# Two token streams across the passages between the big products, squares summed on GpSimd, norm roots taken on columns

## What is computed

```python
# two layers i; the context stream xc does the same in layer 0
hl = modulate(rmsnorm(xl, g_pre_mix[i]), ml[0], ml[1])       # before w_in
xl_new = xl + ml[2] * rmsnorm(y_l, g_post_mix[i])             # y_l = merged @ w_o
h2 = modulate(rmsnorm(xl_new, g_pre_mlp[i]), ml[3], ml[4])    # before w_mlp_in ("up")
xl_new = xl_new + ml[5] * rmsnorm(sqrelu_mlp(h2, ...), g_post_mlp[i])
# third block
h = rms_norm(x, norm1_g); z = h @ w_in                        # "win2"
x = x + merged @ w_o                                          # "w_o2"
x = x + peer(rms_norm(x, norm2_g), peer_wq, ...)              # "wq2"
```

## Time and profile before

| | us |
|---|---|
| median of 3 runs | 4296.63 (4293.73 to 4300.03) |
| profiled execution | 4287.48 |
| its span | 4286.2 |
| PE busy | 3978.9 |
| DVE busy | 2143.3 |
| ACT busy | 1532.8 |
| POOL busy | 494.4 |

### The profile page before, as it was taken

How to read it: one execution, slowest core, us unless ns; L and a number is a source line. 1 busy time by engine, 2 the same in 40 slices (tenths; PEclk the granted TensorE clock), 3 DMA queues, 4 the chain that set the end, 5 groups by cost and what they waited for, 6 DMA issues and landing times.

```text
span 4286.2 us, 47339 instructions
## 1 busy us (share of the span) xinstructions
PE 3978.9 (93%) x19554; PEld 3173.2 (74%) x19554; DVE 2143.3 (50%) x3759; ACT 1532.8 (36%) x1878; POOL 494.4 (12%) x748
## 2 busy tenths in 40 slices
PE   6988989999889889998798999999998999999999
PEld 4755768888766668875676877878877788888887
DVE  2165343333447344453353343788883566654444
ACT  3245442212234542234455333344444322222222
POOL 0000000000000000000000100176566111100000
PEclk8999999999999899998899999999999999999999
DMA  5400113332120022222111432344555656643332
GB/s 192 165 8 1 52 70 115 118 109 98 50 81 1 16 74 89 99 79 93 53 47 61 134 109 87 139 155 142 176 167 163 200 182 193 189 143 127 109 117 89
DMA packets 109831, 459.73 MB, mean 107 GB/s; under 512 B 9216, under 2 KB 43120, under 8 KB 68912
## 3 DMA queue, kind: packets, MB, share of 16 engines
q1 hardware_dynamic: 82048, 354.96, 23.8%
q0 software_dynamic: 27568, 101.74, 8.1%
HBM read 389.04 MB, written 67.63 MB: 107 GB/s over the span
## 4 chain that ended last, share of the span: by engine, by line
PE 81%; DVE 7%; ACT 6%; DMA 3%; POOL 2%; issue 2%; SPq 0%; DVEq 0%; ACTq 0%; POOLq 0%
PE ps L538 21%; PE ps L540 21%; PE ps L539 21%; PE ps L951 2%; PE ps L2257 2%; PE ps L618 2%; PE ps L968 1%; POOL Y L2393 1%; PE ps L471 1%; DMA gdram<-GST 1%; DVE MX L1111 1%; PE ps L957 1%; PE ps L1014 1%; DMA stage<-in_w_mod 1%; PE ps L1805 1%
## 5 line engine op out<-in xcount | busy, mean ns | idle before, releaser
L538 PE MATMUL ps<-HH,WH 128*128 128x512 f32 x2760 | 1062.1, 385 | 56.4 <-DVE HL L659 38.0
L539 PE MATMUL ps<-HL,WH 128*128 128x512 f32 x2760 | 1051.9, 381 | 0.0
L540 PE MATMUL ps<-HH,WL 128*128 128x512 f32 x2760 | 1051.6, 381 | 0.0
L445 DVE TENSOR_TENSOR WL<-stage,WH 128x2048 fp32r<-128x2048 f32 x248 | 567.7, 2289 | 488.1 <-ACT WH L434 488.1
L434 ACT ACTIVATE WH<-stage 128x2048 fp32r<-128x2048 f32 x248 | 472.8, 1906 | 589.6 <-PE ps L540 533.3
L538 PEld LDWEIGHTS ps<-HH,WH 128*128 128x128 f32 x2760 | 526.5, 191 | 169.5 <-issue 53.0
L540 PEld LDWEIGHTS ps<-HH,WL 128*128 128x128 f32 x2760 | 526.5, 191 | 106.5
L539 PEld LDWEIGHTS ps<-HL,WH 128*128 128x128 f32 x2760 | 525.8, 191 | 103.6 <-issue 0.7
L538 PE MATMUL ps<-AHp,WH 128*128 128x512 f32 x1024 | 406.8, 397 | 7.3 <-ACT Y L2575 7.3
L539 PE MATMUL ps<-ALp,WH 128*128 128x512 f32 x1024 | 406.6, 397 | 0.0
L540 PE MATMUL ps<-AHp,WL 128*128 128x512 f32 x1024 | 406.5, 397 | 0.0
(11 more groups left out here) (360 smaller groups left out, 5072.2 us busy)
## 6 DMA issues: line engine op xcount, KB each, us to landing
stage<-in_w SPq DMA_DIRECT2D x64, 1024.0 KB, 4.9
stage<-in_u SPq DMA_DIRECT2D x64, 1024.0 KB, 4.9
stage<-in_v SPq DMA_DIRECT2D x64, 1024.0 KB, 4.9
stage<-in_w_mod SPq DMA_DIRECT2D x48, 1024.0 KB, 4.9
GR<-gdram POOLq DMA_DIRECT2D x32, 1024.0 KB, 8.4
adram<-GR SPq DMA_DIRECT2D x22, 1024.0 KB, 4.2
AR<-adram POOLq DMA_DIRECT2D x88, 256.0 KB, 3.5
gdram<-GST SPq DMA_DIRECT2D x16, 1024.0 KB, 5.7
```

Source lines behind the costliest of these rows:

```text
L445: dve.e.tensor_tensor(k.WL[o % 2][:, 0:w], k.stage[n % 2][:, 0:w], k.WH[o % 2][:, 0:w].bitcast(F32), ALU.subtract).then_inc(*dve.done("sla ...
L538: pe.e.matmul(o, wh[:, kk, cs], L.hh[:, kk, z], start=first, stop=False)
L539: pe.e.matmul(o, wh[:, kk, cs], L.hl[:, kk, z], start=False, stop=False)
L540: mm = pe.e.matmul(o, wl[:, kk, cs], L.hh[:, kk, z], start=False, stop=last)
```

## The change

A class `Bridge` describes a passage, and a list of steps (`mlp_steps`, `x_steps`, `p_steps`) gives its order; every engine walks through the same list and does its own part of each step. The tokens go in two streams: latents and context in layer 0, two halves of 256 in layer 1 and later. The last two slabs of the product before (`last=2`) and the first two of the one after (`first=2`) are computed chunk by chunk for one stream, then for the other; `out (c, s)` and `in (c, s)` are such chunks. ScalarE squares as before, but sums of squares go to GpSimd for every norm of the passages (`pool_square_sum`, line 968 of the changed kernel). The statistics are products of the sum with one column of ones, giving a column per 128 tokens (step `stat`, line 869); ScalarE takes one Sqrt over these 2 or 4 columns (`root`, line 898), VectorE the reciprocal, and puts it on a diagonal (`diag`); a product of ones with the diagonal (`rows`, line 874) brings the factors to all partitions in PSUM, where the add and split steps read them. `hi` and `lo` are the splits of the next matrix's slabs. `add (s, c)` multiplies chunk c and adds chunk c - 1; `split` likewise. GpSimd's loads in `pool_heads` wait for the last norm before `win2`. Modulation slabs are not woven into `up`'s group 0, layer 1's scales are computed before the passage into its `w_in`, `HH2` and `HL2` lie elsewhere in SBUF, and the PSUM banks are handed between rings of four double banks and of eight single ones. The core of the diff:

```diff
+STREAMS = [[LAT, CTX], [(0, 256), (256, 256)]]
...
+        def streamed(chunks):
+            for s, z in enumerate(self.streams):
+                for c in chunks:
+                    if any(s0 <= z[0] < s0 + sn for s0, sn in self.segs(c)):
+                        yield (c, s), c, s
+
+        yield from streamed(range(self.first))
+        for c in range(self.first, self.last):
+            yield c, c, None
+        yield from streamed(range(self.last, self.n))
...
-            woven(("up", l, g), 2, lambda s: io["w1"][l, 2 * g + s], rest, lambda s: 1)
+            woven(("up", l, g), 2, lambda s: io["w1"][l, 2 * g + s], rest, lambda s: 1 if g > 0 else 0)
...
+            for i in L.used_after(key):
+                scalar_split(k, act, k.slab_of[L.name, i] + 2)
...
-def vector_square_sum(k, dve, name, c, a, b):
-    t, before = k.TA.of((name, c)), k.TA.of((name, c - 1))
-    dve.wait_ge("square", (name, c))
-    if c > 1:
-        dve.wait_ge("sq_sum", (name, c - 1))
-    dve.e.tensor_tensor(t[:, a:b], t[:, a:b], before[:, a:b], ALU.add).then_inc(*dve.done("sq_sum", (name, c)))
...
+def steps(name, *xs):
+    return [(name, x) for x in xs]
+def add_steps(s, lo=0, hi=9):
+    return steps("add", *[(s, c) for c in range(lo, hi)])
+def split_steps(s, lo=0, hi=9):
+    return steps("split", *[(s, c) for c in range(lo, hi)])
+def second_half(l, adds):
+    y1, n0, n1 = ("y", 1), ("n", 0), ("n", 1)
+    use = lambda *cs: steps("use", *[(c, 0) for c in cs]) if l == 0 else []
+    if l == 0:
+        out = adds[:-2] + steps("stat", y1) + steps("root", y1) + adds[-2:] + steps("hi", 1) + steps("lo", 0)
+        out += steps("diag", y1) + steps("rows", y1) + steps("lo", 1)
+        out += steps("stat", n0) + steps("root", n0) + steps("diag", n0) + steps("rows", n0)
+    else:
+        out = adds + steps("hi", 1) + steps("lo", 0) + steps("stat", n0) + steps("root", n0) + steps("diag", n0)
+        out += steps("stat", y1) + steps("root", y1) + steps("diag", y1) + steps("rows", n0, y1)
+    out += split_steps(0) + steps("in", (0, 0), (1, 0)) + (steps("lo", 1) if l == 1 else []) + add_steps(1)
+    out += use(0, 1) + steps("in", (2, 0)) + steps("stat", n1) + steps("root", n1) + steps("diag", n1) + use(2)
+    return out + steps("in", (3, 0)) + steps("rows", n1) + split_steps(1) + use(3)
+def mlp_steps(l):
+    y0 = ("y", 0)
+    out = steps("out", (4, 0), (5, 0), (6, 0), (7, 0), (4, 1)) + steps("stat", y0) + steps("root", y0) + steps("diag", y0)
+    out += steps("out", (5, 1)) + steps("rows", y0) + steps("out", (6, 1)) + add_steps(0, 0, 3) + steps("hi", 0)
+    return out + steps("out", (7, 1)) + steps("made", 0) + second_half(l, add_steps(0, 3))
+def x_steps(l):
+    y0 = ("y", 0)
+    out = steps("out", *[(c, 0) for c in range(8)], (0, 1), (1, 1)) + steps("stat", y0) + steps("root", y0)
+    out += steps("diag", y0) + steps("out", (2, 1), (3, 1)) + steps("rows", y0)
+    for c in range(4):
+        out += steps("out", (4 + c, 1)) + add_steps(0, c, c + 1) + (steps("hi", 0) if c == 1 else [])
+    return out + steps("made", 0) + second_half(l, add_steps(0, 4))
+def p_steps():
+    n0, n1 = ("n", 0), ("n", 1)
+    out = steps("out", (4, 0), (5, 0), (6, 0), (7, 0), (4, 1)) + steps("stat", n0) + steps("root", n0) + steps("diag", n0)
+    out += steps("out", (5, 1)) + steps("rows", n0) + steps("out", (6, 1)) + steps("hi", 0) + split_steps(0, 0, 2)
+    out += steps("lo", 0) + steps("out", (7, 1)) + steps("made", 0) + steps("hi", 1) + split_steps(0, 2)
+    out += steps("stat", n1) + steps("root", n1) + steps("diag", n1) + steps("lo", 1)
+    return out + steps("in", (0, 0), (1, 0)) + steps("rows", n1) + steps("in", (2, 0)) + split_steps(1) + steps("in", (3, 0))
...
+        elif step == "stat":
+            name, total, sn = B.name(*x), B.sum(*x), B.cols(x[1])[1]
+            p = stats.take(pe, ("norm", name), ("norm_t", (name, 7)))
+            pe.wait_ge("sq_sum", (name, 7))
+            for j in range(sn // 128):
+                mm = pe.e.matmul(p[:, j:j + 1], total[:, 128 * j:128 * j + 128], k.ones[:, 0:1], start=True, stop=True)
+            mm.then_inc(*pe.done("stat", name))
+        elif step == "rows":
+            name, sn = B.name(*x), B.cols(x[1])[1]
+            pe.wait_ge("diag", name)
+            pe.e.matmul(k.psum.of(("norm", name))[:, 0:sn], k.ones[:, :], k.RS.of(name)[:, 0:sn], start=True,
+                        stop=True).then_inc(*pe.done("rows", name))
...
+        elif step == "root":
+            name, m = B.name(*x), B.cols(x[1])[1] // 128
+            r = k.RS.take(act, name, ("rows", name))
+            act.wait_ge("stat", name)
+            act.e.activation(r[:, 512:512 + m], k.psum.of(("norm", name))[:, 0:m], ACT.Sqrt, bias=k.epsc[:, 0:1],
+                             scale=1.0 / 1024).then_inc(*act.done("root", name))
+        elif step == "add" and x[1] > 0:
+            s, c = x[0], x[1] - 1
+            act.wait_ge("x_new", (B.name("y", s), c))
+            scalar_bridge_square(k, act, B, "n", s, c, k.X[:, c, B.cols(s)[0]])
...
+            r, m = k.RS.of(name), sn // 128
+            dve.wait_ge("root", name)
+            dve.e.reciprocal(r[:, 520:520 + m], r[:, 512:512 + m]).then_inc(*dve.done("root_recip", name))
+            dve.wait_ge("root_recip", name)
+            dve.e.tensor_tensor(
+                r[:, 0:sn].rearrange("p (j n) -> p j n", j=m),
+                k.ident[:, :].rearrange("p (o n) -> p o n", o=1).broadcast_to([128, m, 128]),
+                r[:, 520:520 + m].rearrange("p (j o) -> p j o", o=1).broadcast_to([128, m, 128]),
+                ALU.mult).then_inc(*dve.done("diag", name))
+        elif step == "add":
+            (s, c), (z, sn) = x, B.cols(x[0])
+            name = B.name("y", s)
+            if c < 8:
+                t = k.TD.take(dve, (name, c), ("x_new", (name, c)))
+                dve.wait_ge("rows", name)
+                dve.e.scalar_tensor_tensor(t[:, z], k.Y[:, c, z], B.scale[0](c, z.start), k.psum.of(("norm", name))[:, 0:sn],
+                                           ALU.mult, ALU.mult).then_inc(*dve.done("norm_t", (name, c)))
+            if c > 0:
...
+def pool_square_sum(k, pool, name, c, before, total, squares):
+    pool.wait_ge("square", (name, c))
+    pool.wait_ge("square" if before[1] == 0 else "sq_sum", before)
+    pool.e.tensor_tensor(total, total, squares, ALU.add).then_inc(*pool.done("sq_sum", (name, c)))
...
+                  lambda bank: [("y", (l, bank))], True, [4, 5, 6, 7, 0, 1, 2, 3], last=2, streams=STREAMS[l])
...
+                  g == 0, first=2 if g == 0 else 0, streams=STREAMS[l], shared=(l == 1))
...
 def pool_heads(k, pool, io):
     pool.wait_end("layer1", "pe", "dve", "act")
+    pool.wait_ge(*N1_READY)
     pool.e.dma_start(k.cosN[:, :], io["cosN"]).then_inc(*pool.landed("cosN"))
```

More of the change, by code:

```diff
@@ L148, in of, with regroup, __init__ @@
         return self.at.get(key, self.bufs[0])
+def regroup(old, new):
+    ends, order = {}, []
+    for r in old:
+        assert not r.held
+        for i, e in r.free:
+            for b in r.cells[i]:
+                ends[b] = tuple(e)
+                order.append(b)
+        r.free = []
+    for r in new:
+        r.free = sorted(((i, sum((ends[b] for b in r.cells[i]), ())) for i in range(len(r.bufs))),
+                        key=lambda entry: max(order.index(b) for b in r.cells[entry[0]]))
 class Linear:
-    def __init__(self, name, nslab, K, ncol, segs, hh, hl, ready, ends, pair=False, order=None):
+    def __init__(self, name, nslab, K, ncol, segs, hh, hl, ready, ends, pair=False, order=None, first=0, last=0,
+                 streams=(), shared=False):
         self.name, self.nslab, self.K, self.ncol, self.hh, self.hl = name, nslab, K, ncol, hh, hl
@@ L253, in memory @@
     after_h2 = s.at
+    new = s.tensor
     k.cosN = new("cosN", [128, 512])
@@ L302, in memory @@
     k.gin = [new(f"GIN{i}", [128, 512]) for i in range(4)]
+    k.SQp = k.cosN
     g = Room(nc, after_h2)
@@ new lines, in tensor_bridge @@
+def tensor_bridge(k, pe, B, out, into, mark, stats, then=None):
+    for step, x in B.order:
+        if step == "out":
+            next(out)
+        elif step == "in":
+            next(into)
+        elif step == "made":
+            next(out, None)
+            pe.mark(mark)
+            if then:
+                regroup([stats], then)
+                stats = then[0]
+        elif step == "stat":
[10 more added lines that the diff above has]
+                        stop=True).then_inc(*pe.done("rows", name))
@@ new lines, in pool_square_sum, with pool_bridge @@
+def pool_square_sum(k, pool, name, c, before, total, squares):
+    pool.wait_ge("square", (name, c))
+    pool.wait_ge("square" if before[1] == 0 else "sq_sum", before)
+    pool.e.tensor_tensor(total, total, squares, ALU.add).then_inc(*pool.done("sq_sum", (name, c)))
+def pool_bridge(k, pool, B, kind, whole):
+    for step, x in B.order:
+        if step == "out":
+            c, s = x
+            key = kind
```

(10 more changed lines are left out.)

653 lines of the change are left out of this document (424 added, 229 removed).

## The result

The changed kernel takes 4300.76 us (median of 20 runs, 4294.67 to 4306.86), the kernel before 4294.18 in the 20 runs beside it; the ratio is 1.0017 with a 95% interval of 1.001 to 1.0024, so **+6.6 us** by the medians and **+7.3** by the ratio, whose interval is +4.3 to +10.3. The forecast was +8.6, which made 4305 on the earlier median of 4296.63. The profiled execution of the changed kernel ran 4298.74 us, its span is 4297.4: 11.2 more than before's. That is more than the difference of the medians because before's profiled execution happened to lie 6.7 under its median, and the changed kernel's only 2.0 under.

What follows compares the result with a forecast made beforehand. TensorE was busy 3978.9 of 4286.2 us, so only its five passages, costing 142.9 us, could give. Passages -0.7, halved chunks +2.1, waits +4.8, +1.7 and +0.7 made +8.6 us: 4305 from 4296.63, range 4283 to 4325.

Steps and rivals of the forecast that it cites:

- the work behind them: Costs outside the five passages: halved chunks +2.1, layer 1's `w_in` +4.8, its `down` 0 +1.7, `down` 7 +0.7 us.
- B1: Passage from `w_o` to `up` in layer 0: cost 31.2 us after the change, -5.8 to before.
- B2: Passage from layer 0's `down` to layer 1's `w_in`: cost 34.7 us after the change, -3.2 to before.
- B3: Passage from `w_o` to `up` in layer 1: cost 32.3 us against 26.7 before, +5.6.
- B4: Passage from layer 1's `down` to `win2`: cost 34.1 us after the change, +5.7 to before.
- B5: Passage from `w_o2` to `wq2`, with one norm: cost 9.9 us after the change, -3.0 to before.
- wait for slab 2: Layer 1's `w_in`: the slab's split stands behind the streamed slabs' last chunk, leaving TensorE without a slab, +4.8 us.
- halved chunks: 24 chunks of 512 tokens run as two of 2.85 us for 5.60, +0.09 each, +2.1 us.
- Cheap sums: Rival, chance 0.26: GpSimd's sums cheap or not excluding VectorE; at 1.1 us per 512-wide add passages -9.2, total 0; about 4287.
- Dear sums: Rival, chance 0.14: GpSimd's sums exclude VectorE longer; 1.2 us excluded gives total +17, 1.6 gives +33; about 4318 us.
- Clock kept: Rival, chance 0.10: TensorE granted 2.4 GHz throughout, 13 us of slow start and part of the rest gone; -4, 4292 us.
- Cover gone: Rival, chance 0.08: `W1` or a third slab late at one place, +15 us on the forecast sum, 4320 us.

Runs made afterwards that it cites:

- e2: The kernel before with only the weaving changed, no modulation slab behind up's group 0 in layer 0: 4300.63 us, ratio 1.0026 to before.
- e1: The changed kernel with two modulation slabs instead of one woven behind each slab of layer 0's first down group: 4291.5 us, ratio 1.0002 to before.
- e9: e1 with every GpSimd sum followed by a second instruction of its size whose result nobody reads: 4366.28 us, ratio 1.0169 to before.
- e7: e1 with both passages of layer 1 written as before (one stream, VectorE's sums, Ln and Exp): 4281.11 us, ratio 0.9978 to before.
- e3b: The changed kernel with the streams' squares summed by TensorE, GpSimd keeping whole chunks' sums and stream 1's second norm: 4335.1 us, ratio 1.0104 to before.

## Why the forecast came out as it did

**The sum.** +8.6 against +6.6 to +7.3 measured. That it came out so close is luck: four errors of seven to ten us cancel. The passages cost 9.0 less than forecast; the work behind them some 7 more (16 for 9.3); the modulation's closings, put at nothing, +10.4; and the stretches that the change does not touch, also put at nothing, -6.7 in the profiled executions.

**What it missed: the modulation's closings.** The largest of the four has a cause that runs show. The step that failed is the sentence "Nothing for these: ... the mods move under `w_o`'s products". The edit takes two modulation slabs out of `up`'s group 0, and so shifts all later ones by two places: those that close a set, slabs 7 and 23, move from behind `down` slabs, where ScalarE evicts their row at once, behind `up` slabs. e2 shows the effect alone (+11.2), e1 its removal. A moved step costs where it lands: the order of ScalarE's queue around `mrow` would have told it beforehand.

**The passages.** Their cost was forecast at 142.2 and is 133.2. B1: 31.2 forecast, 30.4 measured; B2 34.7, 33.4; B3 32.3, 29.6; B4 34.1, 30.8; B5 9.9, 9.0. (The forecast took off 0.3 to 0.4 us more of products in each passage than its 2.85 and 5.60 a chunk add up to, 1.7 in all, and does not say for what; the measured costs take off 2.85 and 5.60.) The signs are right in all five, with layer 1 slower and the others faster, and the milestones of B3 nearly hold: first next product 26.9 forecast, 26.5 measured; wait for the second norm's sums 7.2 and 5.6; end 66.9 and 63.8. The first of these holds because two errors meet: the last sum comes at 21.4 and not 23.1, but from there to the rows VectorE can read takes 3.4 us (1543.69 to 1547.10) and not 2.3. The main term that was mis-sized is the price of a sum, 0.95 us for 256 columns and 1.45 for 512: instructions of line 968 in the changed kernel (ns min/median/max) take less.

```profile
L968 POOL TENSOR_TENSOR SQ<-SQ,SQU x50: 717/733/2768, 1514.7 to 1958.4; 128x256 f32<-128x256 f32 x50
L968 POOL TENSOR_TENSOR cosN<-cosN,TA x11: 730/736/1301, 2584.5 to 2621.9; 128x256 f32<-128x256 f32 x8, 128x512 f32<-128x512 f32 x3
```

They take 0.73 and 1.30 us. The Trainium skill's figures for a 2048-wide add (GPSIMD Engine Reference, section 3.1), from which the prediction estimated 1.1 us for 512 columns plus a fixed part, agree with the 1.30. The exclusion is real: one 256-wide sum takes 2.768 us, the 0.73 and most of a `WL` split of 2.28 that began just before it. In the timelines it is the first of these two sums, begun at 1535.92, while VectorE splits from 1535.83 to 1538.11:

```profile
1535.92 3.45 POOL L968 TENSOR_TENSOR SQ<-SQ,SQU 128x256 f32<-128x256 f32 x2 [1.49 <-ACT SQU L882]
...
1535.83 2.28 DVE L506 TENSOR_TENSOR WL<-stage,WH 128x2048 fp32r<-128x2048 f32 x1
```

**Behind the passages.** Forecast +9.3, measured some 16: e1's row of the table sums to +6.7, with -9.7 of it inside the passages. The wait for slab 2 in `w_in` is 4.63, forecast 4.8; but TensorE ran at 1.2 GHz for 6.8 us behind it, a loss of 3.4 that the forecast did not count. Into `down` 0 of layer 1 the wait is 2.2 us (forecast 1.7), released by the slab's `WL` split, which stands behind two of the relu and split steps that the forecast named; `down` 7 waits 0.7 (forecast 0.7). With the 2.1 for halved chunks, which no run measures by itself, these make 13.0; some 3 us of the 16 are not assigned.

**The rivals.** Cheap sums: this rival was the nearer one in the passages. The price was 0.73, not 0.95, and they came out at -9.7 to before, where its first figure was -9.2; by itself that would have made the total about 0, had the other errors not stood against it. Its sign, a last sum before 21, just failed at 21.4. Its far end, -24.5 for VectorE's own price without exclusion, is not what the chip did (1.30 us for 512 columns, and the exclusion is there); no run shows what such sums would give. Dear sums: e9 shows the slope steeper than forecast, 72 for 40. The forecast treated one price as a straight slope. The second norm suggests a corner: its seven sums follow VectorE's adds at 0.87 us a step in the changed kernel, and come at 1.6 to 1.8 a step in e9. Clock kept: refuted, the gaps stand at 0.56 to 0.79 and the chunks behind them at 0.83 to 0.95. Cover gone: the loads of `cosN` to `W1` stayed hidden; `W1`, issued at 1976.0, landed 15.1 us later and was first read at 2008.0. e1 and e7, with and without the streams in layer 1, differ by 10.3 us, of which their rows of the table have 9.7 in its two passages.

## What to carry to other kernels

Halving a stretch of work to hide one half's norm under the other's products pays where the products are long beside the vector work (768 tokens, or one norm instead of two), and loses where the half chunk is shorter than the steps that it should cover: the same edit gave -5.3 us and +6.7 us in two passages of one kernel, and in a third (B2, also 768 tokens) a gain of 4.5 us in the passage went in the wait for a slab behind it, so measure such an edit place by place. Whatever an edit moves, follow to where it lands, also what only slides along in a list behind it. And the releaser that the profile names tells which queue ended last, not what its removal gives: ScalarE ended level with GpSimd here, and the engine that took over the sums was no earlier. Test the price from both sides, and ask of the cheaper side what the replacement costs.

## What the hardware did that I had not expected

The 3.5 us that TensorE waited for one row of modulation cost more than their length: its granted clock fell to the 1.2 GHz level for 6.8 us from the end of the first such wait (754.2 to 761.0) and for 3.4 us at the second, though it had been fully busy for over 100 us before. By the starts of the slab splits the first wait cost 5.9 us. And TensorE's products of one column are not small: with a weight load of 0.19 us each at full clock they took 0.11 us from start to start among other products and 0.21 at the 1.2 GHz level behind an idle stretch, so that in e3b a half chunk of 1.42 us grew to 1.87.
